# Half-wide buffers for expert outputs, the lower half added inside the down product, and one more down row block held in the freed columns

## The reference

```python
def block(args):
    tids, e, w = args
    xb = x_pad[tids]
    hdn = jax.nn.silu(xb @ w1[e]) * (xb @ w3[e])
    return (hdn @ w2[e]) * w[:, None].astype(xb.dtype)

y = lax.map(block, (slot_tok.reshape(n_blocks, MOE_BLOCK), block_exp,
                    slot_w.reshape(n_blocks, MOE_BLOCK)))
out = jax.ops.segment_sum(y.reshape(P, D), slot_tok, num_segments=N + 1)[:N]
```

## Time and profile before

| | us |
|---|---|
| median of 3 runs | 1484.53 |
| lowest, highest | 1483.81, 1484.76 |
| the profiled execution: its own time | 1488.51 |
| the profiled execution: its span | 1486.4 |

### The profile page before, as it was taken

How to read it: one execution, slowest core, us unless ns; L and a number is a source line. 1 busy time by engine, 2 the same in 40 slices (tenths; PEclk the granted TensorE clock), 3 DMA queues, 4 the chain that set the end, 5 groups by cost and what they waited for, 6 DMA issues and landing times.

```text
span 1486.4 us, 19397 instructions
## 1 busy us (share of the span) xinstructions
PE 1452.9 (98%) x7786; PEld 885.1 (60%) x7786; DVE 559.9 (38%) x1162; ACT 472.9 (32%) x838; POOL 150.4 (10%) x136
## 2 busy tenths in 40 slices
PE   8999999999999999999999999999999999999998
PEld 6766544544544445987545445444453786888886
DVE  6775111111111113047211211111111588689965
ACT  4561111111111113454111111111111572676654
POOL 0211000000000002962000000000000710001200
PEclk9999999999999999999999999999999999999999
DMA  8658999999999999838999999999999846554410
GB/s 307 246 235 303 407 421 429 427 426 428 428 428 428 425 423 389 309 122 350 404 412 429 428 427 428 427 426 429 426 425 409 325 170 227 186 211 170 174 53 29
DMA packets 82597, 503.35 MB, mean 339 GB/s; under 512 B 5200, under 2 KB 10960, under 8 KB 55632
## 3 DMA queue, kind: packets, MB, share of 16 engines
q1 hardware_dynamic: 81792, 497.67, 82.4%
q0 software_dynamic: 576, 4.19, 0.7%
q10 hardware_dynamic: 144, 0.26, 0.0%
HBM read 501.05 MB, written 1.05 MB: 338 GB/s over the span
## 4 chain that ended last, share of the span: by engine, by line
PE 87%; DMA 6%; DVE 3%; ACT 2%; issue 1%; SPq 1%; POOL 0%; DVEq 0%; ACTq 0%
PE bank L1212 27%; PE bank L1259 14%; PE bank L1064 9%; PE bank L1157 8%; PE bank L1572 6%; DMA ring<-in_w_up 4%; PE bank L1600 4%; PE bank L1171 3%; PE bank L1574 3%; PE bank L971 2%; PE bank L990 2%; PE bank L908 1%; DMA ring<-in_w_in 1%; PE bank L1227 1%; PE bank L1095 1%
## 5 line engine op out<-in xcount | busy, mean ns | idle before, releaser
L1212 PE MATMUL bank<-ring,arena 128*64 128x512 f32 x1280 | 281.9, 596 | 6.2 <-issue 4.0
L1212 PEld LDWEIGHTS bank<-ring,arena 128*64 128x64 f32 x1280 | 94.9, 138 | 188.1 <-issue 186.9
L1212 PE MATMUL bank<-arena 128*64 128x512 f32 x576 | 167.8, 592 | 0.0
L2278 DVE TENSOR_TENSOR arena<-arena,bank 128x512 f32<-128x512 f32 x32 | 22.0, 688 | 370.5 <-PE bank L1212 370.5
L1259 PE MATMUL bank<-ring,arena 128*64 128x512 f32 x640 | 141.7, 595 | 2.4 <-ACT arena L1760 2.4
L1572 PE MATMUL bank<-x_split,w_high 128*128 128x512 f32 (+1 forms) x408 | 138.7, 391 | 0.2 <-DVE x_split L2081 0.2
L1157 PEld LDWEIGHTS bank<-SEL,x_by_row 128*128 128x128 f32 x1024 | 116.7, 192 | 25.8 <-issue 24.3
L2297 DVE SCALAR_TENSOR_TENSOR y_low<-bank,ST,y_high 128x512 fp32r<-128x512 f32 x64 | 48.0, 751 | 202.5 <-ACT y_high L1764 202.5
L1157 PE MATMUL bank<-SEL,x_by_row 128*128 128x128 f32 x1024 | 122.8, 278 | 0.0
L1764 ACT ACTIVATE y_high<-bank,ST 128x512 fp32r<-128x512 f32 x64 | 44.0, 687 | 245.7 <-PE bank L1259 245.7
L1212 PEld LDWEIGHTS bank<-arena 128*64 128x64 f32 x576 | 54.8, 137 | 106.3 <-issue 106.3
(11 more groups left out here) (387 smaller groups left out, 2213.0 us busy)
## 6 DMA issues: line engine op xcount, KB each, us to landing
ring<-in_w_gate SPq DMA_DIRECT2D x32, 2048.0 KB, 25.5
ring<-in_w_up SPq DMA_DIRECT2D x32, 2048.0 KB, 22.5
ring<-in_w_down SPq DMA_DIRECT2D x32, 2048.0 KB, 22.7
arena<-in_w_gate SPq DMA_DIRECT2D x18, 2048.0 KB, 21.6
arena<-in_w_down SPq DMA_DIRECT2D x16, 2048.0 KB, 23.7
arena<-in_w_up SPq DMA_DIRECT2D x14, 2048.0 KB, 16.5
ring<-in_ffn_up SPq DMA_DIRECT2D x12, 2048.0 KB, 9.0
ring<-in_w_in SPq DMA_DIRECT2D x8, 2048.0 KB, 15.6
```

Source lines behind the costliest of these rows:

```text
L1212: last = nc.tensor.matmul(bank[4 + m][64 * e:64 * e + 64, :], XG[:, c, 64 * e:64 * e + 64], w[e][:, c, :], start=(c == 0), stop=(c == C - 1))
```

## The change

Each of `y_high` and `y_low` becomes 512 columns wide and holds one half of the outputs at a time. `scatter` takes a half: the upper half (1) of pair n is still added in pair n + 1, at step 4, with 4 products. The lower half (0) of pair n is added in pair n itself, with 4 products that stand between the last two products of step 6: after (half 1, j = 3, e = 0) and before (half 1, j = 3, e = 1). They wait for `y_copied` of half 0. This holds for the 15 pairs with `next_pair`. In pair 15 the half 1 goes to two further buffers over XG. The 1024 freed arena columns (SPARE_ROW) hold row block 0 of matrix 46; it is loaded at `n == POOL` in one more transfer, behind the three others, and the later load of matrix 46 shrinks from 1280 to 256 columns.

```diff
-        YHI, YLO = part("y_high", "arena", 2304, [P, D]), part("y_low", "arena", 3328, [P, D])
+        YHI, YLO = (part(name, "arena", 2304 + 512 * n, [P, 512])[:, :] for n, name in enumerate(("y_high", "y_low")))
+        LAST_YHI, LAST_YLO = (part(name, "arena", 512 * n, [P, 512])[:, :]
+                              for n, name in enumerate(("last_y_high", "last_y_low")))
+        SPARE_ROW = cut(3328, D)
...
-                        for to, end in ((SPARE_END, SLOT // 2), (SPARE_MID, SLOT // 2 - 512)):
+                        for to, end in ((SPARE_END, SLOT // 2), (SPARE_MID, SLOT // 2 - 512), (SPARE_ROW, SLOT // 4)):
...
-                        words = slice(0, SLOT // 2 - 768 if n == SPARE_N else SLOT)
+                        words = slice(SLOT // 4 if n == SPARE_N else 0, SLOT // 2 - 768 if n == SPARE_N else SLOT)
...
-            def scatter(s, n):
+            def scatter(s, n, half):
 
                 pe.wait_ge(s["swt_copied"], n + 1)
-                pe.wait_ge(s["y_copied"], n * 2 + 2)
+                pe.wait_ge(s["y_copied"], n * 2 + half + 1)
                 for t in range(T):
-                    for half in range(2):
-                        for y in (YHI, YLO):
-                            last = nc.tensor.matmul(bank[2 * t + half][:, :], SWT[:, t, :],
-                                                    y[:, 512 * half:512 * half + 512],
-                                                    start=False, stop=False, skip_group_check=True)
+                    for y in (YHI, YLO):
+                        last = nc.tensor.matmul(bank[2 * t + half][:, :], SWT[:, t, :], y,
+                                                start=False, stop=False, skip_group_check=True)
                 return last
...
                 if next_pair and not first:
-                    scatter(s, n - 1)
+                    scatter(s, n - 1, 1)
...
+                    if j == 0:
+                        return [(slice(0, 512), SPARE_ROW[:, cols_])]
...
                 def down(half, js):
                     for j in js:
                         for e in range(2):
+                            if next_pair and (half, j, e) == (1, FE // P - 1, 1):
+                                scatter(s, n, 0)
                             for to, rows_ in down_pieces(e, j, half):
```

More of the change, by code:

```diff
@@ L1179, in scatter_by_half @@
                 for half in range(2):
-                    for y, ready in ((YHI, moe["y_high"]), (YLO, moe["y_copied"])):
+                    for low, ready in enumerate((moe["y_high"], moe["y_copied"])):
                         pe.wait_ge(ready, n * 2 + half + 1)
@@ L1183, in scatter_by_half @@
                             last = nc.tensor.matmul(bank[2 * t + half][:, :], SWT[:, t, :],
-                                                    y[:, 512 * half:512 * half + 512],
+                                                    ((YHI, YLO), (LAST_YHI, LAST_YLO))[half][low],
                                                     start=False, stop=False, skip_group_check=True)
-                            if y is YLO and half:
+                            if low and half:
                                 last.then_inc(acc_done, 1)
@@ L1246, in down_pieces @@
                     cols_ = slice(512 * half, 512 * half + 512)
-                    if spare_ready is None or e != SPARE_N % 2 or j == 0:
+                    if spare_ready is None or e != SPARE_N % 2:
                         return [(slice(0, 512), w[e][:, j, cols_])]
+                    if j == 0:
+                        return [(slice(0, 512), SPARE_ROW[:, cols_])]
                     if j >= FE // P // 2:
@@ L1284, in experts @@
                 if last_of is not None:
-                    scatter(s, n).then_inc(last_of, 1)
+                    scatter(s, n, 1).then_inc(last_of, 1)
             def moe_layer(l, name):
@@ L1359, in moe_layer @@
                             first=(p == 0), up_free=None if p else (flag_ready, l + 1),
-                            spare_ready=(spare_loaded, 16 * (6 * l + 3)) if p == SPARE_N // 6 else None,
+                            spare_ready=(spare_loaded, 16 * (7 * l + 4)) if p == SPARE_N // 6 else None,
                             up_rows=([as_expert(FIRST[HALVES_N % POOL - RING + k], 2 + k) for k in range(2)],
-                                     (spare_loaded, 16 * (6 * l + 5))) if p == HALVES_N // 6 else None)
+                                     (spare_loaded, 16 * (7 * l + 6))) if p == HALVES_N // 6 else None)
                     if p == 0:
@@ L1763, in experts @@
                     act.wait_ge(s["y_done"], n * 2 + half + 1)
-                    nc.scalar.activation(YHI[:, 512 * half:512 * half + 512], bank[6 + half][:, :], ACT.Copy,
-                                         scale=slot_gate).then_inc(s["y_high"], 1)
+                    high = YHI if next_pair or not half else LAST_YHI
+                    nc.scalar.activation(high, bank[6 + half][:, :], ACT.Copy, scale=slot_gate).then_inc(s["y_high"], 1)
             def first_tokens(s, g):
@@ L2138, in expert_center @@
             def expert_center(l, t):
-                dve.wait_ge(spare_loaded, 16 * (6 * l + 6))
+                dve.wait_ge(spare_loaded, 16 * (7 * l + 7))
                 for n in range(2):
@@ L2294, in experts @@
                 for half in range(2):
-                    cols_ = slice(512 * half, 512 * half + 512)
+                    high, low = (YHI, YLO) if next_pair or not half else (LAST_YHI, LAST_YLO)
                     dve.wait_ge(s["y_high"], n * 2 + half + 1)
-                    v.scalar_tensor_tensor(YLO[:, cols_], bank[6 + half][:, :], slot_gate, YHI[:, cols_].bitcast(F32),
+                    v.scalar_tensor_tensor(low, bank[6 + half][:, :], slot_gate, high.bitcast(F32),
                                            ALU.mult, ALU.subtract).then_inc(s["y_copied"], 1)
```

## The result

| | us |
|---|---|
| before, median of 5 runs (lowest, highest) | 1484.76 (1483.81, 1487.78) |
| changed, median of 5 runs (lowest, highest) | 1513.44 (1513.01, 1514.97) |
| ratio, 95% interval | 1.0189 (1.0178 to 1.0201) |
| the profiled execution of the changed kernel: own time, span | 1514.97, 1512.8 |

The change costs 28.7 us where 23.2 were forecast (by the interval of the ratio, 26.4 to 29.8). The time lies inside the range of 1494 to 1514, at its upper end, and above the narrower 1504 to 1511 that was thought most likely.

A forecast was written before the change was run, and what follows sets the result against it. PE sets the MoE layers' 27.03 us period, transfers nearly level. Adding 1.08 us a pair, 16.4 a layer, less spare time of 5.1 and 4.0, gives +11.3 and +12.4; less 0.5, +23.2 on 1484.5: 1507.7 us, range 1494 to 1514.

The forecast's parts named there:

- the narrower 1504 to 1511: Whole kernel: times thought most likely, from 0.95 to 1.2 us added a pair; chance 0.72.
- the third rival: Start of the down product: the hidden rows' copy or weight-load order exposes 0.2 us more a pair, 1514 us; chance 0.08.
- the cover of the hidden rows' copy: Ahead of the down product: four scatter products still hide ACT's copy of HT, by 0.15 us.
- the lost slot: End of the down product: the lone leftover product makes 25 slots of 24, +0.857 us a pair.
- The spare time as the measure: Both MoE layers: only PE time added beyond 5.1 us in layer 0 and 4.0 in layer 1 moves the end.
- The split pair: Last two down products, parted by the scatter: a lone one costs 0.857 us a pair, bounds 0.43 and 0.89.
- the two rivals that spare the slot or half of it: Leftover down product: it slides past the scatter, some 1483.5 us, chance 0.12; or costs 0.43, 1495 us, chance 0.08.
- The changes of shape: Between 64-column and 128-column products: one more change there and back, 0.22 us a pair, bounds 0.1 and 0.3.
- the four moved products: Scatter products moved from the next pair's step 4 to this pair's step 6: no net PE cost, 0.97 us moved.
- The wait for `y_copied`: Ahead of the lower-half scatter: no cost in ordinary pairs, 0.2 us in pair 0, once a layer.
- What follows the layers: After layer 1: early weights end the wait of PE's transposes for ACT's casts, giving back 0.5 us.
- The load: Early row block load at pairs 0 and 1: counted at nothing, bounds -1.2 and +1; later slot freeing opens dips.

The follow-up runs named there:

- e1: Changed kernel with the four lower-half scatter products one product earlier, ahead of (half 1, j = 3, e = 0): 1491.58 us, ratio 1.0034.
- e8: Kernel before plus one small full-width f32 product ahead of (half 1, j = 3, e = 1) in pairs 0 to 14: 1518.29 us, ratio 1.0216.
- e9: Kernel before plus the small product of e8 one place earlier, ahead of (half 1, j = 3, e = 0): 1493.90 us, ratio 1.0047.
- e2: Changed kernel with the scatter in two groups of two, ahead of (half 1, e = 1) at j = 2 and j = 3: 1527.46 us, ratio 1.0273.
- e5: The kernel before run once more without any edit, with a profile of its own: 1485.61 us, ratio 0.9994.
- e4: e1 without the early load of row block 0 of matrix 46: 1491.41 us, ratio 1.0035 to before.
- e6: e1 with half-wide buffers in pairs 0 to 7 only, wide buffers and the old scatter from pair 8 on: 1488.28 us, ratio 1.0011 to before.
- e7: e6 without the early load of the row block: 1492.05 us, ratio 1.0036 to before.
- e3: Changed kernel without the early load of row block 0 of matrix 46: 1513.35 us, ratio 1.0186 to before.

## Why the prediction was right, and where it was off

**The range.** Its upper end, 1514, was set by the third rival, in which the cover of the hidden rows' copy fails. That did not happen (below). The time came to that end by other terms, each small and all but one in the same direction, so that it still fell inside is in part luck. The deciding term, the lost slot, was right in kind and size.

**The spare time as the measure.** Right. Everything that PE got on top of its spare time went through to the end: no wait of PE for weights is left in the changed kernel, as the list of PE's waits shows. The longest that bear on the change:

```profile
PE bank L891 <- issue: 2.6, 2, 1.6
PE bank L1264 <- ACT arena L1765: 2.4, 4, 0.7
```

**The split pair.** The term of 0.857 us measured 0.83, twice independently (changed against e1, e8 against e9). The choice between 0.43 and 0.89 was right, and so was the count of slots instead of torn products (e2). By it the two rivals that spare the slot or half of it fall: with the 0.36 that e1 shows for the rest, nothing for the slot would make the period 27.39 and 0.43 would make it 27.82, and it is 28.22.

**The changes of shape and the four moved products.** Together these two terms were mis-sized: 0.22 was taken for the first (bounds 0.1 and 0.3) and nothing for the second, and 0.36 was measured (27.39 - 27.03 in e1). The timeline of pair 2 shows where the rest is. The changes themselves are as forecast. The entry costs 0.09 us as in the earlier trace rows; the way out 0.10, as the last scatter product (226.16) is 0.33 ahead of the leftover product (226.49) where scatter products follow each other by 0.23; the longer first slot (226.49 to 226.97, 0.48 instead of 0.43) 0.05. That is 0.24, the sum that the prediction rounded down to 0.22 for a saving that is not seen. The rest is inside the group: its first product is 0.34 ahead of the second (225.36, 225.70), 0.11 more than the 0.23 of the others. This step needs no change of shape. The kernel before has it too, where the scatter stands behind full-width transposes: its first product starts at 212.68, and then

```profile
213.00 0.39 PE L1171 MATMUL bank<-y_low,chosen_t 128*128 128x512 f32 x1
213.23 0.40 PE L1171 MATMUL bank<-y_high,chosen_t 128*128 128x512 f32 x1
```

The group of eight pays it once. The change makes two groups of four, and the upper one pays it at the old place (217.03 to 217.35, 0.32) and the lower one again. So four of eight do not cost half of 1.93 us: the upper four take 218.04 - 217.03 = 1.01. "Cost PE nothing net" is where the prediction was off, by 0.11 a pair. Why a group's first product is slow was not tried. With it, 0.09 + 0.10 + 0.05 + 0.11 = 0.35, against 0.36 between the periods. Slot and the rest together are 0.83 + 0.36 = 1.19 us a pair where 1.08 were taken, and over 15 pairs and two layers that is 0.11 x 30 = 3.3 us. On the Trainium skill's rule (TensorEngine Tiling (Array Packing), Key Properties) that a change of tiling mode drains TensorE, these rows agree, and price it at 0.24 for going there and back.

**The wait for `y_copied`.** In ordinary pairs none, as foreseen. In pair 0 the gap ahead of the scatter is 0.56 us against 0.52 in other pairs, so 0.04 and not 0.2.

**The cover of the hidden rows' copy.** It holds: from the L1234 products (218.04) to the down product (218.35) there is the same 0.31 us as in the earlier trace rows. The third rival did not come about, though its 1514 is close to the time.

**The spare time itself.** 5.1 and 4.0 us were one execution's; e5 has 4.2 and 4.0. This is 0.9 us more on the change.

**What follows the layers.** Here I counted 0.5 us back, and against an ordinary execution it is not there to be had. From the norm's first product behind layer 1 (L1095 of the kernel before) to the first product with `in_high` (L908) there are 7.09 us in the profiled execution of before and 6.48 in e5, where ACT's casts were done ahead of PE's transposes without any change. In the changed kernel the casts are early as well, but the same stretch is 7.68 us, since PE itself stops inside these transposes: in the earlier trace rows's place two of eight run at 1184.64, the others only from 1186.00:

```profile
1184.64 0.38 PE L891 MATMUL bank<-KT,X 128*128 128x128 f32 x2
...
1186.00 0.88 PE L891 MATMUL bank<-KT,X 128*128 128x128 f32 x6 [0.98 <-issue]
```

That is 1.2 us more than in e5. The list above has 2.6 us of such waits behind the two layers ("issue", in which the profile shows nothing that PE waits for), the kernel before has 1.4, all of it behind layer 0. The stop behind layer 1 is in all seven programs in which PE sets the layers' ends (the changed kernel, e1 to e4, e8, e9) and in none of the four in which late weights do (before, e5, e6, e7). Why was not tried.

**The load.** Right at nothing where PE sets the period (e3, e4). That the later progress of pairs 0 and 1 opens gaps was right too, and larger than I said. Before, then the changed kernel, at the same places of pairs 1 and 2, counted from their gates: 6 to 9 us behind the first, 0 to 3 us behind the second (last columns PE clock, DMA share, GB/s):

```profile
173.76:176.76 3.00, 3.00 (x16) 1.21 (x14) 0.00 (x0) 0.60 (x1) 0.00 (x0) 1.00 1.14 384
...
194.82:197.82 3.00, 3.00 (x16) 1.00 (x14) 1.64 (x5) 1.97 (x2) 0.00 (x0) 1.00 0.94 350
```

```profile
176.05:179.05 3.00, 3.00 (x16) 1.01 (x14) 0.00 (x0) 0.60 (x1) 0.00 (x0) 1.00 0.75 284
...
198.27:201.27 3.00, 3.00 (x15) 1.05 (x16) 1.15 (x3) 1.88 (x2) 0.00 (x0) 1.00 0.76 202
```

The share is 0.75 and 0.76 where it was full and 0.94. By the count used for e6 the queue loses 7.7 and 6.8 us a layer in the changed kernel, 5.7 and 4.8 in the kernel before. PE never feels it, as it is the slower of the two.

**The sum with the measured terms.** 23.2 + 3.3 (slot and shapes) + 0.9 (spare time) - 0.3 (pair 0's wait) + 0.5 (not given back) + 1.2 (PE's stop) = 28.8 us, against 28.7 measured. That the two agree to 0.1 is luck: the measured difference is good to 1.7 us either way, and the last terms are read from single executions.

## What to carry to other kernels

Half-width products of two streams are free only as a pair. Before a full-width product is put among them, count each stream's products between one full-width block and the next; the longer stream is the time, and a cut after an odd product costs a whole slot each time round. A cut between pairs still costs 0.36 us here: 0.24 for the two changes of shape, and 0.11 because a group of products that is divided pays the slow step after its first product twice. So price a part of a group from the rows of its members, not as its share of the whole. And when transfers look saturated, find out how much PE loses to them by the end of the stage, a low clock behind a wait included: that number, here 4 us in some 420, is all that an edit on PE may cost.

## What the hardware showed beyond that

A short full-width product is not cheap when it stands among half-wide ones: e9 adds one f32 product of 64 columns and the period grows by 0.52 us (27.55 against 27.03). Its two records take 0.36 us up to the next down product (221.60 to 221.96), more than the 0.23 of an fp32r product of 512 columns inside its group. Four such products moved to the same place cost 0.36 beyond their own time. And one group of 408 products in the final block of the same kernel takes 2.3 us more or less from one execution to the next, with the granted clock at 1.00 in both.
